# Parameter and constant tables placed ahead of the activations h_hi and h_lo in SBUF

## The chip, the cores and the metric

The kernel runs on one core of a Trainium2 chip. The metric is the time of one execution on the device, in microseconds. TensorE is called PE here, VectorE DVE, ScalarE ACT, GpSimd POOL, and SyncE, which issues most transfers, SP.

## The reference

Two transformer-like blocks follow each other on 256 tokens of width 2048, all in float32. Cut to what matters:

```
h = rmsnorm(x, norm_mix);  p = h @ w_in            # mixers: pooling, long convolution, gating
x = x + concat(y_a, y_b, y_c) @ w_out
h = rmsnorm(x, norm_ffn);  up = dwconv3(h @ ffn_w_up)
x = rmsnorm(x + (silu(gate) * val) @ ffn_w_down, norm_final)
# second block
h = rms_norm(x, norm_g);   proj = h @ w_in_2       # heads, RWKV, queries, three gates
m = rms_norm(mem);         mk, mv = split(m @ w_mem_kv)
merged = sig(ga)*(ya @ w_up_a) + sig(gb)*(yb @ w_up_b) + sig(gc)*(yc @ w_up_c)
out = x + merged @ w_o
```

## The kernel before

**Precision and units.** Each large product is computed from float32r halves: an operand f is split into hi (ScalarE copies it to float32r) and lo (VectorE takes f minus hi). The product is then three matmuls: w_hi with h_hi, w_hi with h_lo, and w_lo with h_hi. The weights come as 736 units of 512 KB (4 k-tiles by 256 columns). SP loads a unit into one of four raw buffers, ScalarE makes w_hi, VectorE makes w_lo, and TensorE runs 24 matmuls on it: 4 k-tiles, 2 column tiles, 3 products. In each matmul a 128 x 128 tile of the weights is loaded, and a 128 x 256 tile of the activations is the moving operand.

**Names and places.** h_hi and h_lo (lines 183 and 184) hold the normalised activations of the stage, 16 k-tiles of 256 columns, 16 KiB a partition each. They are the moving operand of the first projection (17 groups of four units, from line 465 on), of the feed-forward up-projection (loop at line 573), of the low-rank input, of the head loop and the queries (helper `part`) and of half of the merge loop (line 869). The other moving operands of such products are the mixers' output y_hi and y_lo, the hidden layer m_hi and m_lo, the normalised memory mh_hi and mh_lo, the second block's branches ya_hi and ya_lo (line 870) and the merged mg_hi and mg_lo. These five pairs are placed by hand in an arena that begins at arena_at (line 188), each at a whole number of KiB from it.

**Allocation.** The tiles ahead of the arena are allocated in the order of lines 179 to 186: the rings raw, w_hi and w_lo, four tiles of 4 KiB a partition each, then x, h_hi and h_lo of 16 KiB each, then par, a table of 637 numbers a partition (2548 bytes), and con, a table of 1092 (4368 bytes). par holds the scales and biases that ScalarE and VectorE read one column at a time, con the identity, the masks and the columns of ones that serve as weights. Each tile's start is rounded up to 32 bytes. This puts h_hi at byte 82,048 of a partition, h_lo at 98,432, par at 114,816, con at 117,376, and arena_at at 121,760.

**Order of work.** Every engine has one queue whose order is that of the code; semaphores join them. TensorE waits for `split_done` ahead of each unit and for `bank_read` ahead of each group of four units. Between the units of the head loop stand the small matmuls of the RWKV and attention steps. All lines of TensorE's matmuls are that of the helper `mm`, line 417; line 909 is ScalarE's copy, line 1316 the VectorE subtraction that makes w_lo, line 1362 other VectorE operations on two tensors.

The merge loop, which has two kinds of moving operand in turn:

```
for m3 in range(3):
    group(0, h_hi, h_lo)
    group(1, ya_hi, ya_lo, k0=8 * m3, units=2, ...)
```

Of the kernel before, what the change touches and what calls it, by code (L numbers as in the profile page):

```python
# [26 lines left out]
P = 128  # L27
# [44 lines left out]
NPAR = _at  # L72
# [11 lines left out]
NCONST = _at  # L84
# [82 lines left out]
def build(nc, a):  # L167
    out_ap = a["out"]
    with ExitStack() as ctx:
        def sb(name, shape, dt=F32):  # L170
            return ctx.enter_context(nc.sbuf_tensor(name, shape, dt))
# [8 lines left out]
        w_hi = [sb(f"w_hi{i}", [P, UK, UN], F32R) for i in range(RING)]  # L180
        w_lo = [sb(f"w_lo{i}", [P, UK, UN], F32R) for i in range(RING)]
        x = sb("x", [P, KT, T])
        h_hi = sb("h_hi", [P, KT, T], F32R)
        h_lo = sb("h_lo", [P, KT, T], F32R)
        par = sb("par", [P, NPAR])
        con = sb("con", [P, NCONST])
        arena_at = nc.sbuf_base
        arena_at = (arena_at + 31) // 32 * 32
        usable = nc.sbuf_usable_end - arena_at
# [1949 lines left out]
```

How the kernel before makes its waits and increments, by code:

```python
        @block.gpsimd  # L387
        def _(pool):
            for dst, src in ((feat[:, :], "feat"), (fw1[:, :], "fw1"), (fw2[:, :], "fw2")):
                pool.dma_start(dst, a[src]).then_inc(filt_in, 16)
            pool.wait_ge(landed[1], 16)
            for dst, src in ((fw3[:, :], "fw3"), (decay[:, :, :], "decay"), (dft[:, :, :, :], "dft")):
                pool.dma_start(dst, a[src]).then_inc(tables_in, 16)
            pool.wait_ge(free_early, 1)
            for dst, src in ((ws[:, :, :], "ws"), (pw[:, :, :], "pw"), (bs[:, :], "bs")):
                pool.dma_start(dst, a[src]).then_inc(mixer_in, 16)
            pool.wait_ge(free_inv, 1)
            pool.dma_start(inv[:, :, :], a["inv"]).then_inc(inv_in, 16)
            pool.wait_ge(free_lora, 1)
            pool.dma_start(lora[:, :], a["lora"]).then_inc(lora_in, 16)
            with pool.Fori(0, HEADS_A) as g:
                pool.wait_ge(bias_used, g + 1)
                pool.dma_start(bias_t[:, :], a["bias"][g]).then_inc(bias_in, 16)
            pool.wait_ge(free_mem, 1)
            for c in range(4):
                cs = slice(4 * c, 4 * c + 4)
                pool.dma_start(memx[:, cs, :], a["memT"][:, cs, :]).then_inc(mem_in[c], 16)
# [10 lines left out]
            def unit(bank, k0, hi, lo, first, last, tiles=2, fresh=True):  # L419
                slot = next(slots) % RING
                pe.wait_ge(split_done, n.next("split"))
                o = p2(bank)
                for kk in range(UK):
                    for t in range(tiles):
```

## Time and profile before

| | |
|---|---|
| median of 3 runs | 2538.08 us (2537.49 to 2540.97) |
| profiled execution, span | 2537.8 us; no other time is given for this execution |
| PE busy | 2455.0 us, 97% |
| DVE busy | 1534.1 us, 60% |
| ACT busy | 1185.9 us, 47% |
| mean granted clock of TensorE | 0.985 of full speed |
| moved by DMA | 400.39 MB, mean 158 GB/s |

The span is the time from the first to the last instruction of one profiled execution. Busy times overlap between engines. A matmul's duration overlaps that of its neighbours, so that the start times, in the timeline, tell the rate.

### The profile page before, as it was taken

The numbers are of one execution on the slowest core, as the hardware profiler recorded it, in microseconds if no ns is written. First come the engines' busy times: TensorE is split into PE (matmuls) and PEld (weight loads), VectorE is DVE, ScalarE is ACT, GpSimd is POOL, SyncE is SP. The second block draws the span as 40 slices with busy tenths as digits, with TensorE's granted clock in tenths as the row PEclk, the third lists the DMA queues.
The fourth block names the chain that finished last, engine by engine and source line by source line (L and its number), as shares of the span: only waits on it lengthen the run. The fifth ranks groups of instructions, "written<-read, shape, count | busy, mean of one in ns | idle before, by whom it ended". The sixth has DMA issues, their size and how long they took to land.

```text
span 2537.8 us, 51128 instructions
## 1 busy us (share of the span) xinstructions
PE 2455.0 (97%) x19960; PEld 2413.6 (95%) x19960; DVE 1534.1 (60%) x2050; ACT 1185.9 (47%) x1502; POOL 12.8 (1%) x27
## 2 busy tenths in 40 slices
PE   6999998999999999997899999999999999999999
PEld 6898997999999999996899999999999999999999
DVE  6456566666555666566866666766576454544454
ACT  5343335665434666434444445444465443434433
POOL 0000000000000000000000000000000000000000
PEclk9999898999999999998999999999999999999999
DMA  6353354555554555554333333333355355555554
GB/s 233 130 180 116 129 187 132 188 170 194 183 186 167 183 181 189 179 185 147 117 119 112 109 120 111 119 123 104 118 175 173 125 184 179 185 176 175 184 187 160
DMA packets 110145, 400.39 MB, mean 158 GB/s; under 512 B 12394, under 2 KB 12421, under 8 KB 109904
## 3 DMA queue, kind: packets, MB, share of 16 engines
q1 hardware_dynamic: 108000, 391.00, 46.4%
q0 software_dynamic: 2032, 7.67, 0.9%
q8 instruction: 97, 1.59, 0.3%
q14 instruction: 16, 0.13, 0.0%
HBM read 396.52 MB, written 2.10 MB: 157 GB/s over the span
## 4 chain that ended last, share of the span: by engine, by line
PE 92%; DVE 5%; issue 1%; ACT 1%; DMA 0%; DVEq 0%; SPq 0%; ACTq 0%
PE bank L417 91%; DVE w_lo L1316 1%; ACT w_hi L909 1%; DVE scratch L1365 1%; PE bank L611 0%; DVE s_k L1365 0%; DVE h_lo L1362 0%; DMA x<-in_xT 0%; DVE cum L1362 0%; DVE root L1404 0%; DVE ping L1362 0%; DVE s_t L1362 0%; DVE qr L1807 0%; DVE acc L1362 0%; DVE s_t L1369 0%
## 5 line engine op out<-in xcount | busy, mean ns | idle before, releaser
L1316 DVE TENSOR_TENSOR w_lo<-raw,w_hi 128x1024 fp32r<-128x1024 f32 x736 | 892.0, 1224 | 803.8 <-ACT w_hi L909 797.5
L909 ACT ACTIVATE w_hi<-raw 128x1024 fp32r<-128x1024 f32 x736 | 770.7, 1057 | 1018.7 <-PE bank L417 999.5
L417 PE MATMUL bank<-h_hi,w_hi 128*128 128x256 f32 x4016 | 1163.3, 290 | 36.6 <-DVE h_lo L1362 15.0
L417 PE MATMUL bank<-h_lo,w_hi 128*128 128x256 f32 x4016 | 1141.0, 284 | 0.0
L417 PE MATMUL bank<-h_hi,w_lo 128*128 128x256 f32 x4016 | 1140.8, 284 | 0.0
L417 PEld LDWEIGHTS bank<-h_hi,w_hi 128*128 128x128 f32 x4016 | 775.6, 193 | 47.0 <-issue 24.4
L417 PEld LDWEIGHTS bank<-h_lo,w_hi 128*128 128x128 f32 x4016 | 775.9, 193 | 3.3 <-issue 2.2
L417 PEld LDWEIGHTS bank<-h_hi,w_lo 128*128 128x128 f32 x4016 | 775.0, 193 | 0.0
L417 PE MATMUL bank<-m_hi,w_lo 128*128 128x256 f32 x704 | 197.8, 281 | 0.0
L417 PE MATMUL bank<-m_hi,w_hi 128*128 128x256 f32 x704 | 197.1, 280 | 0.0
L417 PE MATMUL bank<-m_lo,w_hi 128*128 128x256 f32 x704 | 195.7, 278 | 0.0
L417 PEld LDWEIGHTS bank<-m_hi,w_hi 128*128 128x128 f32 x704 | 132.4, 188 | 0.0
L417 PEld LDWEIGHTS bank<-m_lo,w_hi 128*128 128x128 f32 x704 | 132.4, 188 | 0.0
L417 PEld LDWEIGHTS bank<-m_hi,w_lo 128*128 128x128 f32 x704 | 132.2, 188 | 0.0
L417 PE MATMUL bank<-ya_hi,w_lo 128*128 128x256 f32 x384 | 107.9, 281 | 0.0
L417 PE MATMUL bank<-ya_hi,w_hi 128*128 128x256 f32 x384 | 107.6, 280 | 0.0
L417 PE MATMUL bank<-ya_lo,w_hi 128*128 128x256 f32 x384 | 106.8, 278 | 0.0
L1365 DVE SCALAR_TENSOR_TENSOR conv_o<-bank,par,conv_o 128x255 f32<-128x255 f32 x176 | 76.7, 478 | 6.5 <-DVE conv_o L1365 3.3
L417 PE MATMUL bank<-mh_hi,w_hi 128*128 128x256 f32 x256 | 74.5, 291 | 5.1 <-DVE mh_lo L1362 3.4
L417 PEld LDWEIGHTS bank<-ya_hi,w_hi 128*128 128x128 f32 x384 | 72.3, 188 | 0.0
L417 PEld LDWEIGHTS bank<-ya_lo,w_hi 128*128 128x128 f32 x384 | 72.3, 188 | 0.0
L417 PE MATMUL bank<-mh_hi,w_lo 128*128 128x256 f32 x256 | 72.2, 282 | 0.0
(414 smaller groups left out, 2820.2 us busy)
## 6 DMA issues: line engine op xcount, KB each, us to landing
raw<-in_units SPq DMA_DIRECT2D x736, 512.0 KB, 3.4
x<-in_xT SPq DMA_DIRECT2D x4, 512.0 KB, 5.8
memx<-in_memT POOLq DMA_DIRECT2D x4, 512.0 KB, 7.2
out_y<-obuf SPq DMA_DIRECT2D x8, 256.0 KB, 4.3
bias_t<-in_bias POOLq DMA_DIRECT2D x8, 192.0 KB, 2.9
dft<-in_dft POOLq DMA_DIRECT2D x1, 1024.0 KB, 7.6
decay<-in_decay POOLq DMA_DIRECT2D x1, 768.0 KB, 5.6
con<-in_con SPq DMA_DIRECT2D x1, 546.0 KB, 7.8
```

Source lines behind the costliest of these rows:

```text
L417: return pe.matmul(out, lhsT, rhs, start=start, stop=stop, skip_group_check=True)
L909: return act.activation(out, in_, ACT.Copy, scale=scale)
L1316: dve.tensor_tensor(w_lo[slot][:, :, :], raw[slot][:, :, :], w_hi[slot][:, :, :].bitcast(F32), ALU.subtract).then_inc(split_done, 1)
L1365: return dve.scalar_tensor_tensor(out, x_, s, y_, op0, op1)
```

## The change

par and con are allocated ahead of h_hi and h_lo instead of behind them. No instruction is added, removed or reordered. h_hi moves from byte 82,048 to 88,992 and h_lo from 98,432 to 105,376, by 6944 bytes, which is 54 x 128 + 32. par moves from 114,816 to 82,048 and con from 117,376 to 84,608, by 32,768 bytes. arena_at stays at 121,760.

```diff
         x = sb("x", [P, KT, T])
+        par = sb("par", [P, NPAR])
+        con = sb("con", [P, NCONST])
         h_hi = sb("h_hi", [P, KT, T], F32R)
         h_lo = sb("h_lo", [P, KT, T], F32R)
-        par = sb("par", [P, NPAR])
-        con = sb("con", [P, NCONST])
         arena_at = nc.sbuf_base
```

## Rows read from the trace of the kernel before

**Rows 1.** Profile page: span, busy time by engine, chain of waits by engine.
```profile
span 2537.8 us, 51128 instructions
...
PE 2455.0 (97%) x19960; PEld 2413.6 (95%) x19960; DVE 1534.1 (60%) x2050; ACT 1185.9 (47%) x1502; POOL 12.8 (1%) x27
...
PE 92%; DVE 5%; issue 1%; ACT 1%; DMA 0%; DVEq 0%; SPq 0%; ACTq 0%
...
```

**Rows 2.** Stretches: us; busy of PE, PEld, DVE, ACT, POOL; clock; DMA; GB/s.
```profile
...
420.00:640.00 220.00, 220.00 (x1836) 220.00 (x1835) 138.49 (x191) 134.26 (x172) 0.00 (x0) 1.00 0.55 181
655.00:740.00 85.00, 85.00 (x724) 85.00 (x723) 48.89 (x55) 32.44 (x32) 0.00 (x0) 1.00 0.57 187
1400.00:1600.00 200.00, 198.79 (x1675) 196.63 (x1674) 133.34 (x230) 95.76 (x155) 1.64 (x3) 1.00 0.34 113
2445.00:2530.00 85.00, 85.00 (x724) 85.00 (x723) 41.61 (x39) 30.46 (x30) 0.00 (x0) 1.00 0.55 182
...
```

**Rows 3.** Timeline of PE, merge loop: start us, length us, instruction.
```profile
...
2109.78 0.28 PE L417 MATMUL bank<-h_hi,w_hi 128*128 128x256 f32 x1
...
2121.17 0.28 PE L417 MATMUL bank<-h_hi,w_lo 128*128 128x256 f32 x1
2121.29 0.28 PE L417 MATMUL bank<-ya_hi,w_hi 128*128 128x256 f32 x1
...
2126.83 0.28 PE L417 MATMUL bank<-ya_hi,w_lo 128*128 128x256 f32 x1
```

**Rows 4.** Chain that ended last, in order: start us, us, what, count.
```profile
...
1270.87 13.76 PE bank L417 x120
1284.95 6.65 PE bank L417 x56
1298.20 34.92 PE bank L417 x282
1333.77 5.55 PE bank L417 x48
1340.19 5.36 PE bank L417 x44
1345.99 13.76 PE bank L417 x120
...
2129.48 103.30 PE bank L417 x864
...
```

**Rows 5.** Instructions touching w_hi: duration ns min/median/max, first and last start.
```profile
...
L417 PEld LDWEIGHTS bank<-h_hi,w_hi x4016: 186/192/337, 22.8 to 2437.9; 128*128 128x128 f32 x192
L417 PE MATMUL bank<-h_hi,w_hi x4016: 277/283/1202, 22.8 to 2438.0; 128*128 128x256 f32 x192
...
L909 ACT ACTIVATE w_hi<-raw x736: 1038/1059/1091, 15.2 to 2523.4; 128x1024 fp32r<-128x1024 f32 x184
L1316 DVE TENSOR_TENSOR w_lo<-raw,w_hi x736: 1160/1226/1227, 20.4 to 2524.5; 128x1024 fp32r<-128x1024 f32 x184
...
L417 PEld LDWEIGHTS bank<-y_hi,w_hi x256: 188/188/192, 292.7 to 382.8; 128*128 128x128 f32 x128
L417 PE MATMUL bank<-y_hi,w_hi x256: 280/280/284, 292.8 to 382.9; 128*128 128x256 f32 x128
...
L417 PE MATMUL bank<-y_lo,w_hi x256: 278/278/280, 293.0 to 383.1; 128*128 128x256 f32 x128
...
```

**Rows 6.** Profile page, costliest groups: busy us, mean ns, idle before.
```profile
...
L417 PE MATMUL bank<-h_hi,w_lo 128*128 128x256 f32 x4016 | 1140.8, 284 | 0.0
...
```

**Rows 7.** Waits of PE: us in total, times, longest us.
```profile
...
PE bank L417 <- DVE S L1368: 2.8, 7, 0.4
...
```

**Rows 8.** ScalarE writing h_hi, then ya_hi: duration ns min/median/max.
```profile
...
L909 ACT ACTIVATE h_hi<-scratch x12: 1040/1057/1064, 18.9 to 1184.2; 128x1024 fp32r<-128x1024 f32 x12
...
L909 ACT ACTIVATE ya_hi<-yall x6: 1039/1044/1059, 2024.8 to 2029.6; 128x1024 fp32r<-128x1024 f32 x6
...
```

**Rows 9.** Instructions that read par: duration ns min/median/max.
```profile
...
L1365 DVE SCALAR_TENSOR_TENSOR conv_o<-bank,par,conv_o x176: 473/476/485, 413.0 to 1038.8; 128x255 f32<-128x255 f32 x176
...
```

## The prediction

> **What bounds the kernel now.** I read the engine totals and the chain of waits first. TensorE is busy in 97% of the span, and 92% of the chain that ended last is TensorE [rows 1]. The table by stretches says the same of each stage: in the projections (420 to 640 us, 655 to 740, 2445 to 2530) PE is busy in every microsecond, VectorE in 49 to 63% of them, the granted clock is 1.00 (the 2.4 GHz level), and DMA stands at 55 to 57% [rows 2]. So the time is the number of matmuls times the distance at which they start, plus a little waiting.
>
> The next view is therefore the distance between starts. A matmul's own duration (about 280 ns) overlaps its neighbours, so it isn't the price; the distance is. Counts come from the code. In the merge loop a group of 96 matmuls that stream h_hi and h_lo alternates with one of 48 that stream ya_hi and ya_lo, with the same ring of weights, the same other engines and the same microseconds. The h group starts at 2109.78 and has its last start at 2121.17: 11.39 us over 95 steps, 119.9 ns. The ya group runs from 2121.29 to 2126.83: 5.54 us over 47 steps, 117.9 ns [rows 3]. One stretch of the chain checks it: 864 matmuls from 2129.48 in 103.30 us [rows 4] are six h groups and six ya groups, 576 x 0.1200 + 288 x 0.1179 + 0.28 for the last one's length = 103.4.
>
> The other tiles in the arena agree with ya. y_hi's 256 matmuls with w_hi, every third of a row of 768, start from 292.8 to 382.9: 90.1 us over 765 steps, 117.8 ns [rows 5]. In the stretches, 220 us of pure h hold 1836 matmuls, while 85 us of m, or of mg, hold 724 [rows 2]; with the two or so taken off that overlap a stretch's edge this is 120.0 ns against 117.7. The medians show it too: 283 ns for the h matmul, 280 and 278 for y_hi and y_lo; 192 ns for a weight load beside h, 188 beside y, although the weights are the same tiles [rows 5]. h is the only moving operand that is slow.
>
> **Why it can be the address.** What distinguishes h from the rest? Not the accumulator bank: h in the up-projection of the feed-forward block and y both alternate between banks 1 and 0. Not the gap between high and low half: y, like h, has 16 KiB there, and ya has 24. Not the shape. What is left is where it lies. The allocator rounds each tile's start up to 32 bytes; the large tiles before h put it at byte 82,048 of a partition, 0 modulo 128. par (2548 bytes, 2560 rounded) and con (4368) follow, and arena_at is 121,760, 32 modulo 128. All arena tiles lie at whole KiB from it, so y, m, ya, mh and mg are all at 32 modulo 128, and the ring's weights at 0. After the change h_hi starts 6944 bytes later, at 88,992, which is 32 modulo 128: the arena's residue. h_lo goes to 105,376. par and con move down by exactly 32,768, so their residue stays; arena_at stays 121,760.
>
> **The change part by part.** It adds, removes and reorders no instruction, wait or transfer.
> The term that counts: matmuls that stream h. By the groups 4016 of each of three kinds (two of them in [rows 5, 6]), 12,048. The code gives the same: 17 groups of 96 in the first projection, 2112 x 2 in the feed-forward block, 48 for the low-rank input, 3072 in the head loop, 768 in the queries, 2304 in the merge. If each goes from 120.0 to 117.8 ns, TensorE is asked for 12,048 x 2.2 ns = 26.5 us less.
> How much of it reaches the end: where PE is never idle, all of it. The head loop is less clean. One pass takes 75.12 us (1270.87 to 1345.99), and the chain lies on PE for 13.76 + 6.65 + 34.92 + 5.55 + 5.36 = 66.24 of it; the rest goes over short VectorE and ScalarE steps [rows 4]. Matmuls that run beside those steps save nothing: seven passes x 8.9 us / 0.12 us is at most some 520 matmuls, 1.1 us. There are small waits already (seven for S, 2.8 us in all, each up to 0.4) [rows 7], and PE arriving sooner lengthens them; for these and the entry of each stage I take another 0.4 us. Both ends of this term: nothing lost, or all of the loop and the queries lost, 3840 x 2.2 ns = 8.4 us. I take 1.5, because the PE share of these stretches, 198.8 us of 200, is near to that of a pure stretch [rows 2].
> What could be late next: a unit of 24 matmuls shrinks from 2.88 to 2.83 us. Its ScalarE copy (1059 ns) and VectorE subtraction (1226) fit [rows 5], and the m and mg stages already take units at that rate, at 182 to 187 GB/s [rows 2]. So no engine becomes the bound.
> Other instructions that touch h: twelve ScalarE writes of h_hi at 1057 ns (the like write of ya_hi takes 1044) [rows 8], and as many VectorE writes of h_lo. Bounds: 12 x 13 ns = 0.16 us gained, or as much lost, for either engine. I take nothing.
> par and con: 176 taps of VectorE read a scalar from par at 476 ns [rows 9]. Their residue stays; only the coarse place differs. VectorE is not the bound where they stand. If each went from its median to its longest (485 ns), or to its shortest (473), that is 1.6 us more or 0.5 less of VectorE time, under PE. I take nothing, with these as the ends.
> Sum: 26.5 - 1.5 = 25.0 us. The profiled execution has a span of 2537.8 us [rows 1], and the three runs' median is 2538.1, so what lies around the span is within their spread. 2538.1 - 25.0 = 2513.1.
>
> A page of the Trainium skill speaks against this. In "SBUF — State Buffer", section "Who interferes with whom", TensorE has two independent read ports, for the moving operand and for the weights, and never waits for anyone; the same page makes the cost of an access depend on 16-byte lines. Both 0 and 32 are whole lines, so by that page h costs the same at either and the time stays 2538. The trace, 119.9 against 117.9 ns in one loop, shows that some property of an operand's place costs time, which the page doesn't have; it doesn't show which.
>
> **The rivals.**
> A. Region, not residue. h lies wholly below byte 114,816 and every fast tile wholly from 121,760 up, so the trace fits "low is slow" as well (the weights lie low too, so both of TensorE's reads would fall in one region). Against it: y, m, ya and mg lie from the arena's start to over 90 KiB above it at one distance, so it would have to be one step, just between con and h. Then only what of h_lo passes that step gains: at most 6944 of its 16,384 bytes, 6 or 7 of 16 k-tiles in one kind of three, 4016 x 7/16 x 2.2 ns = 3.9 us at the most. Time 2534.2 to 2538.1; I would say 2536.
> B. No effect: the place of h has nothing to do with it, some property of the h groups that I do not see costs the 2 ns. For: I excluded by elimination. Against: bank, gap, shape and neighbours are covered. Time 2538.
> C. Slower: place and residue both act. A row of h is 1024 bytes; from residue 0 it covers 8 blocks of 128 bytes, from residue 32 it covers 9. If a low region costs more than 2.2 ns and the fast arena rows already carry the price of the ninth block, h keeps the region's price and gets the block's as well. It decides as soon as that price is above what TensorE's pipeline hides. The only size for it in the trace is the 2.2 ns difference: + 12,048 x 2.2 ns = 26.5 us, 2564.6. Against it: nothing shows the arena paying for its residue.
> D. The gain is real, but the head loop and queries give theirs back to growing waits: 26.5 - 8.4 = 18.1, 2520. It lies inside the forecast's own range.
>
> **How the numbers follow.** Forecast (with D): 0.70, its own range 2509 (2.4 ns a matmul, nothing lost: 28.9) to 2522. A: 0.12. B: 0.09. C: 0.09. A measurement of this kernel can tell about 0.2%, 5 us, from no change. A and B fall within it, save a little of A that could combine with a partial effect of the residue; so faster 0.73, same 0.18, slower 0.09. The range goes from 2508 to 2538.6: it holds the forecast, A and most of B, and leaves out C and a tail.
>
> **What would show it.** Right: in the merge loop the h group's 95 steps take 11.19 us, not 11.39, as close as ya's; the h medians fall from 283 to 280 and 278 ns and the weight loads beside them from 192 to 188; the stretch of 864 matmuls that took 103.30 us [rows 4] shrinks by 576 x 2.1 ns = 1.2 us; a head pass goes from 75.1 to about 74.4. A shows as h_lo alone changing, and only for its upper k-tiles. B shows as 120.0 everywhere. C shows as about 122. If the distances fall as said and the time doesn't, the waits for VectorE in the head loop must have grown, and my term for them was wrong.

## The result and the profile after

The changed kernel takes 2507.68 us (median of 4 runs, 2505.56 to 2508.11), against 2539.03 for the kernel before (4 runs); the ratio is 0.9869, 95% interval 0.9856 to 0.9883. It is 31.4 us faster, where 25.0 were predicted, and 0.3 us below the low end of the range. The order of the instructions on every engine is the same in both traces.

The profile page of the changed kernel: span, busy times, chain by engine.

```profile
span 2505.9 us, 51128 instructions
...
PE 2418.7 (97%) x19960; PEld 2378.8 (95%) x19960; DVE 1533.2 (61%) x2050; ACT 1186.3 (47%) x1502; POOL 12.8 (1%) x27
...
PE 91%; DVE 5%; issue 1%; ACT 1%; DMA 0%; DVEq 0%; SPq 0%; ACTq 0%
...
```

DVE and ACT are as busy as before, to within 1 us; only PE has less to do, 36.3 us of it [rows 1]. The stretches of the changed kernel, columns as in [rows 2]:

```profile
...
420.00:630.00 210.00, 210.00 (x1802) 210.00 (x1801) 136.34 (x186) 133.65 (x171) 0.00 (x0) 1.00 0.55 185
655.00:740.00 85.00, 85.00 (x731) 85.00 (x730) 50.52 (x58) 32.44 (x31) 0.00 (x0) 1.00 0.55 180
...
2445.00:2500.00 55.00, 55.00 (x469) 55.00 (x469) 24.52 (x23) 18.00 (x17) 0.00 (x0) 1.00 0.50 172
...
```

In a window full of matmuls the step is the length divided by the count, less 2.4 for those that overlap an edge. h goes from 220 / 1833.6 = 120.0 ns [rows 2] to 210 / 1799.6 = 116.7. The stretch from 655 to 740 us is m, whose addresses the change leaves alone: it goes from 117.8 to 85 / 728.6 = 116.7 as well. The last stretch, mg, stays at 117.8.

The merge loop's first pass, in the timeline of PE (start, length, instruction), answers to [rows 3]:

```profile
...
2010.22 0.28 PE L417 MATMUL bank<-h_hi,w_hi 128*128 128x256 f32 x1
...
2021.41 0.28 PE L417 MATMUL bank<-h_hi,w_lo 128*128 128x256 f32 x1
2021.52 0.28 PE L417 MATMUL bank<-ya_hi,w_hi 128*128 128x256 f32 x1
...
2027.06 0.28 PE L417 MATMUL bank<-ya_hi,w_lo 128*128 128x256 f32 x1
...
```

The h group's 95 steps take 11.19 us and ya's 47 take 5.54: 117.8 and 117.9 ns. The second pass of the same loop, in the same trace, with the same instructions at the same addresses, is quicker:

```profile
...
2116.05 0.28 PE L417 MATMUL bank<-h_hi,w_hi 128*128 128x256 f32 x1
...
2127.13 0.28 PE L417 MATMUL bank<-h_hi,w_lo 128*128 128x256 f32 x1
2127.25 0.28 PE L417 MATMUL bank<-ya_hi,w_hi 128*128 128x256 f32 x1
...
2132.73 0.28 PE L417 MATMUL bank<-ya_hi,w_lo 128*128 128x256 f32 x1
...
```

11.08 and 5.48 us, 116.6 ns. So the new place of h doesn't give one step, but one of two, and something other than the addresses decides which. The instructions that touch w_hi, with min/median/max of the duration, answer to [rows 5]:

```profile
...
L417 PEld LDWEIGHTS bank<-h_hi,w_hi x4016: 186/188/337, 23.2 to 2406.0; 128*128 128x128 f32 x192
L417 PE MATMUL bank<-h_hi,w_hi x4016: 277/280/775, 23.2 to 2406.1; 128*128 128x256 f32 x192
...
```

The h matmul's median went from 283 to 280 ns, the weight load beside it from 192 to 188. The chain of waits of the changed kernel, then two further lines of that of the kernel before (start, length, instructions):

```profile
...
389.50 372.30 PE bank L417 x3168
764.96 369.88 PE bank L417 x3168
...
1245.88 13.64 PE bank L417 x120
...
1320.26 13.64 PE bank L417 x120
...
2097.59 102.63 PE bank L417 x864
2202.78 103.56 PE bank L417 x864
...
```

```profile
...
397.34 379.61 PE bank L417 x3168
780.11 379.40 PE bank L417 x3168
...
```

Both halves of the feed-forward block (3168 matmuls) shrink, by 7.3 and 9.5 us; a head pass goes from 75.12 us [rows 4] to 1320.26 - 1245.88 = 74.38. But 864 matmuls of the merge loop take 102.63 us in one pass and 103.56 in another, where they took 103.30 [rows 4]. The merge loop makes four passes of 864 matmuls, and VectorE's w_lo is waited for ahead of the second, third and fourth. The windows over the entry of the second and third, changed kernel first, then before, show what differs (the column behind POOL is the granted clock):

```profile
...
2097.00:2104.00 7.00, 6.41 (x41) 6.42 (x42) 3.17 (x5) 1.69 (x2) 0.00 (x0) 0.76 0.31 104
2202.00:2209.00 7.00, 6.22 (x39) 6.22 (x40) 3.06 (x5) 1.69 (x2) 0.00 (x0) 0.76 0.31 109
...
```

```profile
...
2129.00:2136.00 7.00, 6.53 (x54) 6.54 (x55) 3.67 (x5) 2.17 (x3) 0.00 (x0) 1.00 0.33 111
2235.00:2242.00 7.00, 6.72 (x56) 6.73 (x57) 3.33 (x5) 2.37 (x3) 0.00 (x0) 1.00 0.29 88
...
```

After the wait between passes (2.4 to 2.6 us for w_lo here, 2.3 to 2.5 in the kernel before) the granted clock is 0.76 of full speed over 7 us in the changed kernel, which is the level of 1.2 GHz for nearly half of them, and 1.00 in the kernel before. The fourth pass is like the third. That is 3 x 7 x 0.24 = 5.0 us given back, in this pair of profiled executions; in the second profiled execution of the changed kernel (f4 below) the clock falls at the same three entries.

### The profile page after: what moved, and what is told of

Same layout as the page of the kernel before. It is cut to its first block, busy times and chain, and to the rows that moved or that the text cites. A ratio compares the mean times of both kernels' runs of the same rounds, so it can differ in the third digit from the quotient of the medians.

```text
span 2505.9 us, 51128 instructions
## 1 busy us (share of the span) xinstructions
PE 2418.7 (97%) x19960; PEld 2378.8 (95%) x19960; DVE 1533.2 (61%) x2050; ACT 1186.3 (47%) x1502; POOL 12.8 (1%) x27
## 4 chain that ended last, share of the span: by engine, by line
PE 91%; DVE 5%; issue 1%; ACT 1%; DMA 0%; DVEq 0%; SPq 0%; ACTq 0%
PE bank L417 90%; DVE w_lo L1316 1%; DVE scratch L1365 1%; ACT w_hi L909 1%; PE bank L611 1%; DVE h_lo L1362 0%; DVE s_k L1365 0%; DMA x<-in_xT 0%; DVE cum L1362 0%; DVE root L1404 0%; DVE ping L1362 0%; DVE s_t L1362 0%; DVE qr L1807 0%; DVE acc L1362 0%; DVE s_t L1369 0%
## 5 line engine op out<-in xcount | busy, mean ns | idle before, releaser
L417 PE MATMUL bank<-h_hi,w_hi 128*128 128x256 f32 x4016 | 1151.1, 287 | 38.0 <-DVE h_lo L1362 15.9
L417 PE MATMUL bank<-h_lo,w_hi 128*128 128x256 f32 x4016 | 1128.2, 281 | 0.0
L417 PE MATMUL bank<-h_hi,w_lo 128*128 128x256 f32 x4016 | 1127.4, 281 | 0.0
L417 PEld LDWEIGHTS bank<-h_hi,w_hi 128*128 128x128 f32 x4016 | 762.5, 190 | 48.4 <-issue 22.4
L417 PEld LDWEIGHTS bank<-h_lo,w_hi 128*128 128x128 f32 x4016 | 762.6, 190 | 3.0 <-issue 1.9
L417 PEld LDWEIGHTS bank<-h_hi,w_lo 128*128 128x128 f32 x4016 | 761.8, 190 | 0.0
L417 PE MATMUL bank<-mh_lo,w_hi 128*128 128x256 f32 x256 | 72.7, 284 | 0.0
```

Source lines behind the costliest of these rows:

```text
L417: return pe.matmul(out, lhsT, rhs, start=start, stop=stop, skip_group_check=True)
```

## The experiments

By distance I mean the address of the moving operand less that of w_hi0 (32,896) or w_lo0 (49,280 unless stated), modulo 256. In the kernel before it is 0 for h and 32 for the arena's operands, in the changed kernel 32 for both. "Arena" stands for y, m, mh, ya and mg. Where a kernel moves the arena, the 32-byte tile spare is moved down to make room (`spare = place("spare", [P, 8], 106688)`). The steps in the table are read from all starts in each timeline, over unbroken rows of matmuls.

| kernel | distance h / arena | steps of h | steps of arena | median us | ratio (95%) |
|---|---|---|---|---|---|
| before | 0 / 32 | 120.0 | 117.8 (mh 116.7) | 2539 | 1 |
| changed | 32 / 32 | 116.7, 117.8 | 116.7, 117.8 | 2507.7 | 0.9869 (0.9856 to 0.9883) |
| e1 con first | 32 / 32 | 116.7, 117.8, 120.0 | 116.7, 117.8, 120.0 | 2509.6 | 0.9882 (0.9865 to 0.9898) |
| e2 96 more bytes | 128 / 160 | 118.7, 120.0 | 117.3, 118.7, 120.0 | 2529.8 | 0.9952 (0.9933 to 0.9970) |
| e3 rings moved | 0 / 128 | 120.0 | 118.7 (mh also 120.0) | 2547.5 | 1.0029 (1.0018 to 1.0040) |
| e4 h_hi alone | 32, lo 128 / 160 | 117.8 | 117.3, 118.7, 120.0 | 2529.8 | 0.9962 (0.9947 to 0.9976) |
| f1 | 0 / 0 | 120.0 | 120.0 | 2552.4 | 1.0050 (1.0034 to 1.0067) |
| f2 (256 mod 512) | 0 / 0 | 120.0 | 120.0 | 2553.3 | 1.0054 (1.0037 to 1.0071) |
| f3 | 64 / 64 | 113.3, 117.8 | 113.3, 117.8 | 2512.1 | 0.9897 (0.9877 to 0.9916) |
| f4 changed again | 32 / 32 | 116.7, 117.8 | 116.7, 117.8 | 2506.4 | 0.9872 (0.9856 to 0.9889) |
| g1 | 96 / 96 | 120.0 | 120.0 | 2553.1 | 1.0053 (1.0036 to 1.0070) |
| g2 | 160 / 160 | 117.3, 118.7 | 117.3, 118.7 (mh also 120.0) | 2527.1 | 0.9951 (0.9931 to 0.9972) |
| g3 | 192 / 192 | 113.3, 117.8 | 113.3, 117.8 | 2467.1 | 0.9701 (0.9663 to 0.9738) |
| g4 | 224 / 224 | 118.3 | 118.3 | 2526.7 | 0.9950 (0.9933 to 0.9968) |
| k1 | w_hi 192, w_lo 64 | 113.3 | 113.3 | 2451.5 | 0.9668 (0.9652 to 0.9685) |
| k2 | w_hi 192, w_lo 0 | 117.8 | 117.8 | 2523.9 | 0.9945 (0.9928 to 0.9961) |
| k3 | w_hi 0, w_lo 192 | 117.8 | 117.8 | 2521.9 | 0.9940 (0.9923 to 0.9957) |
| k4 extra matmul | 32 / 32 | 116.7, 117.8 | 116.7, 117.8 | 2520.2 | 0.9931 (0.9914 to 0.9947) |
| l1 | w_hi 64, w_lo 192 | 113.3, 118.9 | 113.3, 118.9 | 2494.8 | 0.9825 (0.9777 to 0.9873) |
| l2 | w_hi 32, w_lo 160 | 118.9 | 118.9 | 2534.9 | 0.9982 (0.9972 to 0.9993) |

In the rows below, 420 to 620 and 800 to 1000 us lie in the two up-projections (h), 660 to 740 in the first down-projection (m).

**e1, con alone ahead of h.**

```diff
         x = sb("x", [P, KT, T])
+        con = sb("con", [P, NCONST])
         h_hi = sb("h_hi", [P, KT, T], F32R)
         h_lo = sb("h_lo", [P, KT, T], F32R)
         par = sb("par", [P, NPAR])
-        con = sb("con", [P, NCONST])
```

> con alone goes ahead of h, par stays behind it. h_hi starts at 86,432 and h_lo at 102,816, 4384 bytes up instead of 6944; both at 32 modulo 128; the arena stays at 121,760. Residue theory: the same as the changed kernel, h matmuls 116.7 or 117.8 ns apart, no 120.0, about 2507 us. Region theory (what lies below about 114.8 KB of the partition is slow, above it fast): h_lo passes it with only 4384 bytes, h_hi not at all, so at least 85% of the h matmuls stay at 120.0 and the time is over 2530. A theory that it is the place of par, not of h: par is behind h as before, so about 2538.

Its median is the changed kernel's within the noise, although h has moved by 4384 bytes and not 6944. Its four runs are 2515.6, 2509.8, 2509.1 and 2509.4; the profiled one is the slowest, and in it a step of 120.0 shows too. Columns as in [rows 2]; the second stretch is mg:

```profile
...
420.00:620.00 200.00, 200.00 (x1717) 200.00 (x1716) 129.77 (x178) 126.49 (x161) 0.00 (x0) 1.00 0.56 188
2440.00:2500.00 60.00, 60.00 (x502) 60.00 (x502) 28.64 (x26) 21.90 (x21) 0.00 (x0) 1.00 0.57 190
...
```

h has 200 / 1714.6 = 116.6, mg 120.0. Neither the size of the shift, nor the place of par, nor the share of h above 114,816 matters; and a distance of 32 allows 120.0 as well.

**e2, the changed kernel with 96 bytes more.**

```diff
         con = sb("con", [P, NCONST])
+        h_pad = sb("h_pad", [P, 24])
         h_hi = sb("h_hi", [P, KT, T], F32R)
...
-        arena_at = (arena_at + 31) // 32 * 32
+        arena_at = (arena_at - 32 + 127) // 128 * 128 + 32
```

> The changed kernel with 96 unused bytes between con and h: h_hi at 89,088, h_lo at 105,472, both 0 modulo 128, 96 bytes above their place in the changed kernel; the arena starts at 121,888, again 32 modulo 128. Residue theory: h back at 120.0 ns, m, y and ya at 116.7 or 117.8, time 2537 to 2540. Region theory: nothing changes against the changed kernel, about 2508.

```profile
...
420.00:620.00 200.00, 200.00 (x1669) 200.00 (x1668) 126.98 (x176) 122.73 (x158) 0.00 (x0) 1.00 0.57 183
800.00:1000.00 200.00, 200.00 (x1688) 200.00 (x1687) 127.49 (x174) 123.43 (x158) 0.00 (x0) 1.00 0.56 184
...
```

Neither time was met. h ran at 200 / 1666.6 = 120.0 in the first half and 200 / 1685.6 = 118.7 in the second. h was here at distance 128, and that is not the same as distance 0: the modulus 128 of my argument was too small. The region theory, which expected nothing to change, fails on the first half.

**e3, everything from the rings to h up by 32 bytes, order of the kernel before.**

```diff
+        ring_pad = sb("ring_pad", [P, 8])
         raw = [sb(f"raw{i}", [P, UK, UN]) for i in range(RING)]
```

> Order of the kernel before, with 32 unused bytes ahead of the weight rings: raw, w_hi, w_lo, x and h all move up by 32 bytes, so the weights and h both lie at 32 modulo 128, and the arena (121,888) also. Theory A, the moving operand's own residue decides (0 slow, 32 fast): h is fast, 116.7 or 117.8 ns, about 2508 us. Theory B, the difference between the weights' residue and the moving operand's decides (equal is slow): h stays at 120.0, and m, y, ya and mg, which now also share the weights' residue, slow from 117.8 to 120.0: 4800 x 2.2 ns = 10.6 us more than before, and mh 768 x 3.3 ns = 2.5 us; about 2551.

```profile
...
420.00:620.00 200.00, 200.00 (x1669) 200.00 (x1668) 125.38 (x172) 122.02 (x157) 0.00 (x0) 1.00 0.56 182
660.00:740.00 80.00, 80.00 (x677) 80.00 (x676) 45.08 (x49) 29.93 (x29) 0.00 (x0) 1.00 0.58 188
...
```

h is at 160 modulo 256 here, exactly as in the changed kernel, where it had 116.7; but the weights have moved with it, and it has 120.0. So its own residue doesn't decide; the distance from the weights does. The arena, expected at distance 0 by a modulus of 128, is at 128, and has 80 / 674.6 = 118.6, so the time stays below the 2551 that was worked out with 120.0. There is a second pair: this arena (at 32 modulo 256) and e2's h (at 0) differ in their own residue and share the distance of 128, and both show 118.7 and 120.0. e3 is the only run in which the w_hi tiles themselves lie at another residue.

**e4, h_hi alone moved.**

```diff
+        hi_pad = sb("hi_pad", [P, 8])
         h_hi = sb("h_hi", [P, KT, T], F32R)
+        lo_pad = sb("lo_pad", [P, 24])
         h_lo = sb("h_lo", [P, KT, T], F32R)
```

> Order of the kernel before; h_hi alone at 32 modulo 128 (82,080), h_lo at 0 (98,560), arena at 32 (121,888). Two of every three h matmuls stream h_hi. If each matmul pays for its own moving operand, two steps in three are fast and one is slow: two thirds of the changed kernel's 31 us, about 2518. If one slow matmul in three holds the whole stream at the slow rate, about 2538. If what matters is that h_lo and h_hi differ, it could be as fast as the changed kernel, 2508.

```profile
...
420.00:620.00 200.00, 200.00 (x1700) 200.00 (x1700) 128.28 (x178) 125.73 (x161) 0.00 (x0) 1.00 0.56 186
660.00:740.00 80.00, 80.00 (x669) 80.00 (x668) 43.46 (x48) 29.74 (x28) 0.00 (x0) 1.00 0.56 185
...
```

h has 117.8, m 120.0. The time is none of those expected, in part because the arena has gone from 32 to 160 with it. It doesn't tell the theories apart.

**f1 and f2, every distance 0 or 256.** The next kernels all have the changed kernel's order and an unused tile between con and h_hi, with the arena right behind h_lo; f1 has 224 bytes, f2 480, f3 288.

```diff
         con = sb("con", [P, NCONST])
+        h_pad = sb("h_pad", [P, 56])      # f2: 120, f3: 72
         h_hi = sb("h_hi", [P, KT, T], F32R)
```

> The changed kernel with 224 unused bytes between con and h: h_hi at 89,216 and the arena at 121,984. The distance from w_hi0 (32,896) to every moving operand of a weight matmul is then 0 modulo 512. Theory B2 (a moving operand whose distance from the weights is a multiple of 512 can run at no other step than 120.0 ns): all 17,616 such matmuls at 120.0, so 4800 x 2.2 ns for m, y, ya, mg and 768 x 3.3 for mh more than before, 13 us: about 2552. Region theory: h is even higher in the partition than in the changed kernel, so 2508. Theory P (the step is only the phase in which a stream was entered, addresses do nothing): a mix of 116.7, 117.8 and 120.0, between 2505 and 2540, with a wide spread over the runs.

> As the run with all distances at 0, but 480 unused bytes: every distance from the weights is 256 modulo 512. If the modulus that counts is 128 or 256 this is the same case as 0, about 2552, all at 120.0. If it is 512 or more, it is another case, and the step is one of 116.7 to 118.5: 2505 to 2530.

f1 (h, m), then f2 (m):

```profile
...
420.00:620.00 200.00, 200.00 (x1670) 200.00 (x1668) 125.19 (x172) 121.83 (x156) 0.00 (x0) 1.00 0.56 181
660.00:740.00 80.00, 80.00 (x670) 80.00 (x668) 45.03 (x48) 29.47 (x29) 0.00 (x0) 1.00 0.57 185
...
```

```profile
...
660.00:740.00 80.00, 80.00 (x669) 80.00 (x668) 45.35 (x49) 30.07 (x29) 0.00 (x0) 1.00 0.55 185
...
```

h and m are all at 120.0 (200 / 1667.6 and 80 / 667.6 in f1, 80 / 666.6 in f2; a count can be off by one), and the times are 2552.4 and 2553.3, where 2552 was worked out. h lies higher in the partition than in the changed kernel and is slow: this ends the theory of the region. f2 shows that the modulus is at most 256, e2 that it is more than 128 (distances 0 and 128 don't have the same steps).

**f3, distance 64.**

> 288 unused bytes: every distance is 64 modulo 512. If only distances of 0 modulo 128 are bad, it is as good as the changed kernel or better, 2500 to 2515. If the modulus is 64, it is about 2552.

As good as said, but with a surprise in the chain, two passes of the merge loop:

```profile
...
2107.66 98.20 PE bank L418 x864
2208.45 103.55 PE bank L418 x864
...
```

98.20 us for 864 matmuls is 113.3 ns a step behind the first few; in the pass behind it, at the same addresses, it is 117.8 (and an entry at the lower clock).

**f4, the changed kernel itself.**

> The changed kernel itself, unaltered, for the spread of its executions. Theory of the phase (two steps, 116.7 and 117.8 ns, at the same addresses, chosen as a stream is entered after a wait): another profiled execution shows another division of the stages between 116.7 and 117.8, and times between 2505 and 2515. If the address alone sets the step: the same stages at the same steps, 2507 to 2508.

y and mg in the changed kernel's first trace, then in this one:

```profile
...
290.00:370.00 80.00, 80.00 (x688) 80.00 (x688) 50.24 (x54) 30.38 (x29) 0.00 (x0) 1.00 0.56 188
2415.00:2495.00 80.00, 80.00 (x681) 80.00 (x680) 40.00 (x38) 30.18 (x29) 0.00 (x0) 1.00 0.56 184
...
```

```profile
...
285.00:365.00 80.00, 80.00 (x681) 80.00 (x681) 48.92 (x52) 30.72 (x30) 0.00 (x0) 1.00 0.57 188
2412.00:2492.00 80.00, 80.00 (x688) 80.00 (x688) 41.41 (x39) 30.29 (x29) 0.00 (x0) 1.00 0.58 189
...
```

In one execution y has 80 / 685.6 = 116.7 and mg 117.8; in the other y has 117.8 and mg 116.7. The same program takes either step in the same stage. The four runs go from 2504.3 to 2509.2.

**g1 to g4, distances 96, 160, 192 and 224** (unused tiles of 320, 384, 416 and 448 bytes).

> All weight matmuls' moving operands (h, y, m, mh, ya, mg) at distance 96 modulo 256 from the weights. So far: distance 0 gives one step, 120.0 ns; 32 gives 116.7 or 117.8 (once 120.0); 64 gives 117.8 or 113.3. Theory D (the distance modulo 256 sets which steps are possible, the entry into a stream picks one): a set of one to three steps again, held between pauses; whether 113.3 is among them is open. If all do 113.3, about 2552 - 17,616 x 6.7 ns = 2434, if half do, 2475; if 117.8, 2512. A theory that only distance 0 is bad and all others alike: 2505 to 2515 and steps of 116.7 and 117.8.

> Distance 160 modulo 256. The kernel with h_hi alone moved had its arena at this distance and ran there at 120.0, 118.7 or 117.3 ns. Theory D: these steps for all, time between 2520 (mostly 117.3) and 2552 (all 120.0). Theory that all distances but 0 are alike: 2505 to 2515.

> Distance 192 modulo 256, the mirror image of 64. If the modulus is really 128, it is the case of 64: steps 117.8 and 113.3, 2512. If it is 256 and the sign counts, other steps. If the sign doesn't count, 2512 again.

> Distance 224 modulo 256, the mirror image of 32. If the modulus is 128, it is the case of 96; if the sign of the distance doesn't count, it is the case of 32, 116.7 and 117.8 ns, about 2507.

g1 is as slow as distance 0. g2 has the steps that were named. g4 has one step of its own, 118.3, which neither of its two theories had. g3 has the set of 64, but takes the fast one far more often, so that it is at 2467.1 and not the 2512 expected; the two up-projections of one execution:

```profile
...
420.00:620.00 200.00, 200.00 (x1701) 200.00 (x1699) 128.07 (x178) 124.56 (x160) 0.00 (x0) 1.00 0.55 188
800.00:1000.00 200.00, 200.00 (x1767) 200.00 (x1766) 133.61 (x187) 130.01 (x167) 0.00 (x0) 1.00 0.58 195
...
```

200 / 1698.6 = 117.7 and 200 / 1764.6 = 113.3. "All distances but 0 are alike" is wrong. 64 and 192 have the same set of steps, but 96 and 224, 32 and 160 do not, so the modulus isn't 128 here either.

**k1 to k3, w_lo moved against w_hi.** k1 has 128 unused bytes between the rings and a distance of 192 to w_hi:

```diff
+        w_pad = sb("w_pad", [P, 32])      # k2: 48, k3: 16
         w_lo = [sb(f"w_lo{i}", [P, UK, UN], F32R) for i in range(RING)]
         x = sb("x", [P, KT, T])
         par = sb("par", [P, NPAR])
         con = sb("con", [P, NCONST])
+        h_pad = sb("h_pad", [P, 72])      # k2: 56, k3: 104
         h_hi = sb("h_hi", [P, KT, T], F32R)
```

> As the run with all distances at 192, with 128 unused bytes between the w_hi and w_lo rings: distance 192 to w_hi and 64 to w_lo. Both distances gave steps of 113.3 and 117.8 by themselves. If each matmul's step depends only on the distance to the weights being read beside it, 113.3 and 117.8 again, 2457 to 2475. If w_hi and w_lo have to be alike, other steps, above 2500.

> Distance 192 to w_hi and 0 to w_lo. One weight load in three is then at the bad distance. If the cost is paid by load, a step of (113.3 x 2 + 120) / 3 = 115.6 to (117.8 x 2 + 120) / 3 = 118.5 ns: 2480 to 2530. If one bad load holds the whole stream: 120.0, 2552. If w_lo doesn't matter: 2467.

> The opposite: distance 0 to w_hi and 192 to w_lo. Two weight loads in three are at the bad distance. Cost by load: (120 x 2 + 113.3) / 3 = 117.8 or up to 119.3 ns, 2513 to 2540. One bad load holds the stream, or w_hi alone matters: 120.0, 2552.

k1 in the first up-projection, and the second pass of its merge loop:

```profile
...
420.00:620.00 200.00, 200.00 (x1767) 200.00 (x1767) 133.58 (x187) 129.77 (x167) 0.00 (x0) 1.00 0.59 195
...
```

```profile
...
2052.81 99.85 PE bank L419 x864
...
```

864 matmuls take 99.85 us, with an entry at the lower clock in it, where the kernel before took 103.30 [rows 4]. k1 is the version that beats both kernels: every stream of weight matmuls, in every stage, at 113.3 ns once it is under way, and 2451.5 us, 3.3% under the kernel before. I had expected the mixture of g3. k2 in the same stretch:

```profile
...
420.00:620.00 200.00, 200.00 (x1701) 200.00 (x1700) 128.44 (x178) 125.79 (x161) 0.00 (x0) 1.00 0.56 186
...
```

k3 has 1700 matmuls there. Both have 117.8 throughout, so both weight tiles take part: with one of the two at distance 0 the stream never shows the 113.3 that it has with both at 192, and it is faster than the 120.0 with both at 0. Both times lie within what was expected of a price by load (2480 to 2530, 2513 to 2540). But with 113.3 for a good load that price is 115.6 ns for one bad load in three and 117.8 for two in three; that the two kernels have the same step speaks against it.

**k4, the changed kernel with one small matmul more.**

```diff
                     for b in (1, 0):
+                        mm(banks[5][:, 0:64], con_("ident"), con_("upper_eq"))
                         group(b, h_hi, h_lo, ready=(dve_for_pe, quarters) if b else None)
```

> The changed kernel with one more small matmul (con, 128 x 64, into a bank that is not in use there) ahead of each of the 44 up-projection groups; its result is read by no one. No address differs. Theory of the entry: the step of a stream is picked as it starts, so the up-projection, which ran at 116.7 throughout in both profiled executions of the changed kernel, now shows 117.8 in some or all of its groups, and the down-projection behind it follows the last group. If the addresses alone pick the step, all stays at 116.7 and the time is 2507 plus 44 x 0.1 to 0.3 us, 2511 to 2520.

```profile
...
420.00:620.00 200.00, 200.00 (x1718) 200.00 (x1717) 127.24 (x175) 124.51 (x158) 0.00 (x0) 1.00 0.55 182
...
```

The 1718 count the extra matmuls too (the trace has two records for each); by the starts between them the up-projection stays at 116.7. Each extra matmul delays the stream by 0.22 us in the timeline, 10 us for the 44, of the 12.5 by which the median is longer than the changed kernel's. The theory of the entry missed: a small matmul ahead of a stream didn't change its step. But it left no pause either, as the starts around it are at most 0.2 us apart, so it doesn't test what a real wait does.

**l1 and l2, the pair turned round, and another pair 128 apart** (k1 with an h_pad of 160 and 128 bytes).

> Distance 64 to w_hi and 192 to w_lo. If the gap of 128 between the weight rings fixes the stream at its faster step: 113.3 throughout, about 2451. If the pair counts in its order: 113.3 and 117.8 mixed as in the runs with all distances at 64 or 192, 2460 to 2512.

> Distance 32 to w_hi and 160 to w_lo. If the gap of 128 alone gave 113.3: 2451. If each load pays for its own distance: between the steps of 32 (116.7, 117.8) and 160 (117.3, 118.7), 2505 to 2525.

```profile
...
420.00:620.00 200.00, 200.00 (x1685) 200.00 (x1684) 127.93 (x177) 124.17 (x159) 0.00 (x0) 1.00 0.55 181
800.00:1000.00 200.00, 200.00 (x1767) 200.00 (x1766) 132.16 (x184) 130.14 (x167) 0.00 (x0) 1.00 0.59 191
...
```

These are l1's. It has 118.9 in one up-projection and 113.3 in the other, and its runs spread from 2482.9 to 2508.5: neither 113.3 throughout nor the mixture with 117.8 that was expected. l2 has 118.9 everywhere, and at 2534.9 us it is slower than either of its distances alone (2507.7 and 2527.1) and outside both times expected. So the gap of 128 alone doesn't make k1 fast, and the two distances don't add up load by load.

## Why the prediction was wrong

The direction held, and so did the reason in the main: the place of h costs time. The size did not.

**Right.** That h paid more than the other moving operands for where it lies: confirmed by e1 (another shift, same distance, same time) and by f1 (the arena put at h's distance pays the same, 13 us more, as worked out). Of the observations named for it these came: 95 steps in 11.19 us, medians of 280 and 188 ns, a head pass of 74.4 us. One did not: the stretch of 864 matmuls was to shrink by 1.2 us and went from 103.30 to 102.63 in one pass and to 103.56 in the next. No engine became the bound: at 113.3 ns a step k1 still has PE at 96% of the span.

**The step that failed** is "each goes from 120.0 to 117.8 ns". I took the arena's step in the trace of before for the price of its address. Of the h matmuls in unbroken rows, some 10,800, about 70% were at 116.7 in the changed kernel and 30% at 117.8. That makes the term 12,048 x (0.70 x 3.3 + 0.30 x 2.2) = 36 us, not 26.5: 3.0 ns a matmul, where even the fast end of my range had 2.4. And m, y and a quarter of ya went from 117.8 to 116.7 with no change of address, 3168 x 1.1 = 3.5 us, which the prediction did not have at all. The hint was in the trace of before: mh, at the same distance as y and m, already had 116.7 there, 94 steps in 10.97 us:

```profile
...
1926.35 0.28 PE L417 MATMUL bank<-mh_lo,w_hi 128*128 128x256 f32 x1
...
1937.32 0.28 PE L417 MATMUL bank<-mh_hi,w_lo 128*128 128x256 f32 x1
...
```

I had looked at four arena operands that agreed (ya, y, m and mg) and left out the one that didn't.

**The loss of 1.5 us** was too small as well. At the steps it had, the span should have fallen by some 36 + 3.5 = 39.5 us; it fell by 31.9, seven to eight less. Where one and the same matmul starts in the two traces tells where the rest went. The merge loop gave 4.8 us less than its steps are worth; that is the clock at the entry of its passes, 5.0 by the windows. From the low-rank input to the queries it is 3.6 us less. Of these, 2.3 lie in seven passes of the head loop, which gave 5.2 us where 2688 matmuls, about half at either step, are worth 7.5. The chain there has steps of other engines beside PE, as argued for rival D, at a quarter of D's full price; that they are the cause isn't shown. Another 1.4 us went where mh begins, and the first projection and the feed-forward block gave back 1.9 more than their steps. At mh too it is the clock that differs between the two executions. The stretch over its start, before, then changed:

```profile
...
1894.00:1926.00 32.00, 26.88 (x205) 26.16 (x205) 23.47 (x30) 20.86 (x22) 0.00 (x0) 0.95 0.42 141
...
```

```profile
...
1862.00:1895.50 33.50, 28.11 (x208) 27.38 (x206) 23.73 (x31) 20.87 (x22) 0.00 (x0) 0.90 0.40 135
...
```

The prediction had no term for the clock at all. The step's error and the loss's had opposite signs, and it is luck that the sum missed by only 6.4 us.

**Rivals.** A, the region: refuted by f1 and f2, and by e1. B, no effect of the place: refuted by e1 and f1. C, slower by a block more per row: refuted, h at distance 32 is not slower. D, all of the head loop and the queries lost, 8.4 us: about 3.6 were, the low-rank input included. The residue modulo 128 that I argued with is not quite the quantity: e3 shows that it is the distance from the weights, e2 and f2 that it counts modulo 256. In this change both name the same.

The Trainium skill's page "SBUF — State Buffer", section "Who interferes with whom", gives TensorE two independent read ports and says that it never waits on anyone. These runs disagree as far as the effect goes, and the measurement decides: with the same instructions the step lies between 113.3 and 120.0 ns, and the distance between the moving operand and the weights sets which steps occur.

**Open.** What picks a step out of a distance's set. It is not the addresses (f4, the passes of the merge loop, g3's two halves). In the traces it holds as long as a stream runs. Each of the 20 has ten rows of over 120 weight matmuls without a pause; in the 16 traces in which h and the arena share a distance the step never changes inside such a row, and in the other four it changes only where the moving operand does. It changes behind a pause, which fits a lock between the two reads that is caught at the entry; that is argued, and k4, which was to show it, did not. Nor do I have a rule that gives the set from the distances; the table is measured, not derived. That two reads meet in the same part of SBUF is argued from the distance alone, no run shows the meeting.

## What to carry to other kernels

Where TensorE is the bound and hardly ever idle, as here, compare the distance between starts of matmuls that are alike but for their operands; a per cent or two of difference there can be the address of one against the other, and unused bytes between tiles are cheap to try. Try several distances, for moving operand against each weight tile, and don't take one trace's step for the price of an address: look for a second step in the same trace and run each version more than once. Here the placements tried came out between 0.5% slower and 3.3% faster than the kernel before.

## What was not expected of the hardware

- The step of a 128 x 128 by 128 x 256 float32r matmul has a small set of values, 113.3, 116.7, 117.3, 117.8, 118.3, 118.7, 118.9 and 120.0 ns, and keeps one for hundreds of microseconds (2112 h matmuls and 1056 of m behind them in one row at 116.7).
- The granted clock fell to 0.76 over 7 us behind waits of 2.4 to 2.6 us in the changed kernel and stayed at 1.00 behind waits of 2.3 to 2.5 us in the kernel before. Neither the wait's length nor the step decides it alone: in f1, at 120.0 ns, it fell behind a wait of 2.3 us; in g1, at 120.0 as well, it stayed behind 2.7 us; in g2 it fell behind 2.1 us (the three rows below, in this order). Yet the faster streams lose it more often. Over the three entries of all 20 traces it fell at 29 of the 31 behind a pass with a step of 117.8 ns or less, and at 12 of the 29 behind a slower one. So a part of what a faster step saves was lost at the entries. What makes the difference was not tried.

```profile
...
2137.00:2144.00 7.00, 6.44 (x41) 6.45 (x42) 3.35 (x5) 1.69 (x2) 0.00 (x0) 0.76 0.29 109
...
```

```profile
...
2137.00:2144.00 7.00, 6.44 (x53) 6.45 (x54) 3.44 (x5) 2.08 (x3) 0.00 (x0) 1.00 0.29 91
...
```

```profile
...
2109.00:2116.00 7.00, 6.54 (x42) 6.54 (x43) 3.62 (x5) 1.69 (x2) 0.00 (x0) 0.76 0.32 113
...
```
